# Second layer: queries' rms scale applied to the scores by row, keys' sums of squares as two fp32r products

## The reference

```python
for g, (window, dilation) in enumerate(B_PATTERNS):      # 3 groups
    q = apply_partial_rotary(rms_norm(qkv[:, :, 0, g], q_gain[g]), cos, sin)
    k = apply_partial_rotary(rms_norm(qkv[:, :, 1, g], k_gain[g]), cos, sin)
    o, lse = dilated_window_attention(q, k, qkv[:, :, 2, g], window // dilation, dilation)
...
wgt = jax.nn.softmax(jnp.stack(lses), axis=0)
y = o.reshape(bsz, S, B_WIDTH).astype(h.dtype) * jax.nn.silu(z)
```

## Time and profile before

| | |
|---|---|
| Median of 3 runs | 3209.98 us (3209.97 to 3212.14) |
| The profiled execution | 3211.42 us, of which its span 3209.7 us |
| PE busy | 98% |
| POOL, DVE, ACT busy | 49%, 50%, 34% |
| Second layer in the trace | about 425 to 1012 us |
| Mean granted clock of PE | 0.993 |

### The profile page before, as it was taken

How to read it: one execution, slowest core, us unless ns; L and a number is a source line. 1 busy time by engine, 2 the same in 40 slices (tenths; PEclk the granted TensorE clock), 3 DMA queues, 4 the chain that set the end, 5 groups by cost and what they waited for, 6 DMA issues and landing times.

```text
span 3209.7 us, 39426 instructions
## 1 busy us (share of the span) xinstructions
PE 3135.8 (98%) x16286; PEld 2596.1 (81%) x16286; DVE 1619.7 (50%) x2100; ACT 1106.7 (34%) x1509; POOL 1568.7 (49%) x1138
## 2 busy tenths in 40 slices
PE   8999999999999999999999999889999999999998
PEld 7988878788887888898887888766888777778887
DVE  6753565748373535345356777745121366551123
ACT  3221244444443322332223444434222343242222
POOL 4444466658473555444433422236454565345444
PEclk9999999999999999999999999999999999999999
DMA  5554422222222333255443211112323242213231
GB/s 168 164 171 142 139 92 76 79 66 79 74 85 63 95 101 97 92 171 180 135 158 128 66 40 40 40 48 84 105 92 96 89 142 81 79 62 96 92 105 66
DMA packets 279172, 319.33 MB, mean 99 GB/s; under 512 B 6850, under 2 KB 245073, under 8 KB 278674
## 3 DMA queue, kind: packets, MB, share of 16 engines
q1 hardware_dynamic: 240960, 247.48, 23.8%
q10 hardware_dynamic: 38034, 69.34, 6.3%
HBM read 310.50 MB, written 6.29 MB: 99 GB/s over the span
## 4 chain that ended last, share of the span: by engine, by line
PE 89%; DVE 5%; ACT 2%; POOL 2%; issue 1%; DMA 1%; ACTq 0%; SPq 0%; DVEq 0%
PE ps L550 25%; PE ps L551 25%; PE ps L552 25%; PE psx L755 1%; PE psx L1034 1%; POOL Wl L358 1%; PE ps L1065 1%; PE psx L734 1%; PE psx L649 1%; DVE tmp L1908 1%; PE psx L701 1%; PE psx L1193 1%; DVE stD L2282 1%; PE psx L797 1%; PE psx L795 0%
## 5 line engine op out<-in xcount | busy, mean ns | idle before, releaser
L358 POOL TENSOR_TENSOR Wl<-Wr,Wh 128x512 fp32r<-128x512 f32 x928 | 1282.8, 1413 | 1426.0 <-ACT Wh L1281 1421.9
L550 PE MATMUL ps<-Ah,Wh 128*128 128x512 f32 x1944 | 778.2, 400 | 0.7 <-POOL Wl L358 0.7
L552 PE MATMUL ps<-Ah,Wl 128*128 128x512 f32 x1944 | 757.7, 390 | 0.0
L551 PE MATMUL ps<-Al,Wh 128*128 128x512 f32 x1944 | 757.2, 390 | 0.0
L1281 ACT ACTIVATE Wh<-Wr 128x2048 fp32r<-128x2048 f32 x232 | 442.9, 1909 | 285.4 <-DMA Wr<-in_w_mlp_in_dram 109.9
L550 PEld LDWEIGHTS ps<-Ah,Wh 128*128 128x128 f32 x1944 | 365.2, 188 | 83.5 <-issue 9.2
L551 PEld LDWEIGHTS ps<-Al,Wh 128*128 128x128 f32 x1944 | 365.2, 188 | 82.1 <-issue 8.9
L550 PE MATMUL ps<-Yh,Wh 128*128 128x512 f32 x1088 | 426.3, 392 | 5.2 <-POOL Wl L358 5.2
L552 PEld LDWEIGHTS ps<-Ah,Wl 128*128 128x128 f32 x1944 | 364.8, 188 | 77.3
L551 PE MATMUL ps<-Yl,Wh 128*128 128x512 f32 x1088 | 424.3, 390 | 0.0
L552 PE MATMUL ps<-Yh,Wl 128*128 128x512 f32 x1088 | 424.3, 390 | 0.0
(11 more groups left out here) (399 smaller groups left out, 3907.7 us busy)
## 6 DMA issues: line engine op xcount, KB each, us to landing
Wr<-in_a_w_in_dram SPq DMA_DIRECT2D x48, 1024.0 KB, 6.6
modw<-in_w_mod_dram ACTq DMA_DIRECT2D x96, 512.0 KB, 5.5
Wr<-in_b_w_in_dram SPq DMA_DIRECT2D x40, 1024.0 KB, 5.0
Wr<-in_w_mlp_in_dram SPq DMA_DIRECT2D x32, 1024.0 KB, 5.6
Wr<-in_w_mlp_out_dram SPq DMA_DIRECT2D x32, 1024.0 KB, 5.1
Wr<-in_a_w_out_dram SPq DMA_DIRECT2D x16, 1024.0 KB, 5.2
Wr<-in_c_w_in_dram SPq DMA_DIRECT2D x16, 1024.0 KB, 5.7
Wr<-in_attn_w_qkv_dram SPq DMA_DIRECT2D x12, 1024.0 KB, 5.1
```

Source lines behind the costliest of these rows:

```text
L358: last = pool.tensor_tensor(E.Wl[:, s, part], E.Wr[:, s, part], E.Wh[:, s, part].bitcast(F32), ALU.subtract)
L550: pe.matmul(o, ah, bh, start=first, stop=False)
L551: pe.matmul(o, ah, bl, start=False, stop=False)
L552: return pe.matmul(o, al, bh, start=False, stop=last)
```

## The change

Queries are no longer scaled by their root mean square before the scores. ACT writes tile times gain straight into `QB`. The scale is a number per token, and the tokens of the queries are the rows of the scores, so it multiplies the scores by row. For that, the sums of squares are made in four blocks of 32 output partitions, one for each quarter of the tokens (one root for 128 columns instead of 512), a transpose (`columns`) puts tokens on the partitions, and DVE's `rate` takes the reciprocal of 4 columns into `stB`. In `scores`, three products by group replace the one instruction (the scale differs by group), and the maximum is an instruction of its own.

Keys keep their scale. Their squares are rounded to fp32r on ACT (`sh`), DVE subtracts to get the rest (`square_low`), and two fp32r products (high and rest) replace the fp32 product. `rsR` and `sqR` are the memory of `rs` and `sq` under the type fp32r.

DVE's order by step t becomes: `square_low(t)` for a key or `turn(t)` for a query; then, if t - 1 is a key, `scaled(t - 1)` and `turn(t - 1)`; then, if t - 2 is a query, `rate(t - 2)`. The diff, cut to its core:

```diff
+def is_key(t):
+    return t // 2 % 2 == 1
...
         def ssq(i, t):
             r = t % 2
             into(4 + r)
-            pe.wait_ge(*A.of("B", "sq", i, t))
-            pe.matmul(psx[:, r, :], ones[:], sq[:, r, :], start=True, stop=True).then_inc(*X.did("B", "ssq", i, t))
-            emptied[4 + r] = A.of("B", "sqrt", i, t)
+            if is_key(t):
+                pe.wait_ge(*V.of("B", "sl", i, t))
+                for half in (E.rsR, E.sqR):
+                    m = pe.matmul(psx[:, r, :], E.onesR[:], half[:, r, :], start=(half is E.rsR), stop=(half is E.sqR))
+                emptied[4 + r] = A.of("B", "sqrt", i, t)
+            else:
+                pe.wait_ge(*A.of("B", "sq", i, t))
+                for q in range(TT):
+                    m = pe.matmul(psx[32 * q:32 * q + 32, r, 0:P], ones[:, 0:32], sq[:, r, q * P:(q + 1) * P], start=True, stop=True)
+                emptied[4 + r] = V.of("B", "rq", i, t)
+            m.then_inc(*X.did("B", "ssq", i, t))
+
+        def columns(i, t):
+            r = t % 2
+            pe.wait_ge(*A.of("B", "sqrt", i, t))
+            pe.transpose(psx[:, r, P:2 * P], rs[:, r, 0:P], ident[:]).then_inc(*X.did("B", "rt", i, t))
...
             if t:
                 ssq(i, t - 1)
+            if t >= 2 and not is_key(t - 2):
+                columns(i, t - 2)
...
         def sqrt(i, t):
             r = t % 2
+            n = S if is_key(t) else P
             act.wait_ge(*X.of("B", "ssq", i, t))
-            if t >= 2:
+            if t >= 2 and not is_key(t):
                 act.wait_ge(*V.of("B", "qk", i, t - 2))
...
-            act.activation(tmp[:, t % 3, :], ps[t % 3][:], ACT.Copy).then_inc(*A.did("B", "cp", i, t))
+            if is_key(t):
+                n = t // 4 * 2 + t % 2
+                act.wait_ge(*A.of("B", "sq", i, t))
+                act.wait_ge(*X.of("B", "rt", i, t - 2))
+                act.activation(E.rsR[:, t % 2, :], sq[:, t % 2, :], ACT.Copy).then_inc(*A.did("B", "sh", i, t))
...
+                act.activation(tmp[:, n % 3, :], ps[t % 3][:], ACT.Copy).then_inc(*A.did("B", "cp", i, t))
+            else:
...
+                act.activation(E.QB[:, t // 4, t % 2, :], ps[t % 3][:], ACT.Identity, scale=pk(E, "b_q_gain", t // 4)).then_inc(*A.did("B", "cp", i, t))
...
-        def rest(i, t):
+        def square_low(i, t):
+            r = t % 2
+            dve.wait_ge(*A.of("B", "sh", i, t))
+            dve.tensor_tensor(E.sqR[:, r, :], sq[:, r, :], E.rsR[:, r, :].bitcast(F32), ALU.subtract).then_inc(*V.did("B", "sl", i, t))
...
+        def rate(i, t):
+            dve.wait_ge(*X.of("B", "rt", i, t))
+            dve.reciprocal(rq(t // 4, t % 2), psx[:, t % 2, P:2 * P].rearrange("p (q n) -> p q n", q=TT)[:, :, 0]).then_inc(*V.did("B", "rq", i, t))
+
+        def scaled(i, t):
...
+        def turn(i, t):
...
-            dve.tensor_tensor_reduce(PB[:, u % 2, :], psx[:, u % 2, :], maskB[:, u % 4, :], 1.0, 10 * NEG,
-                                     ALU.add, ALU.max, stB[:, u, 0:1]).then_inc(*V.did("B", "sc", i, u))
...
+            for g, c0, c1 in ((0, 0, 256), (1, 256, 384), (2, 384, 512)):
+                dve.scalar_tensor_tensor(PB[:, u % 2, c0:c1], psx[:, u % 2, c0:c1], rq(g, u // 4)[:, u % 4:u % 4 + 1], maskB[:, u % 4, c0:c1],
+                                         ALU.mult, ALU.add).then_inc(*V.did("B", "sc", i, u))
             dve.wait_ge(*V.of("B", "sc", i, u))
+            dve.tensor_reduce(stB[:, u, 0:1], PB[:, u % 2, :], AX.X, ALU.max).then_inc(*V.did("B", "mx", i, u))
...
-            for t in range(11):
-                rest(i, t)
-                if i and t == 1:
+            for t in range(13):
+                if t < 12:
+                    if is_key(t):
+                        square_low(i, t)
+                    else:
+                        turn(i, t)
+                if t and is_key(t - 1):
+                    scaled(i, t - 1)
+                    turn(i, t - 1)
+                if 2 <= t and not is_key(t - 2):
+                    rate(i, t - 2)
+                if i and t == 2:
                     y(i - 1, 1)
-            rest(i, 11)
```

More of the change, by code:

```diff
@@ L216, in setting @@
     E.Wh = sb("Wh", [P, SLOTS, 2048], F32R)
-    E.ones, E.ident = sb("ones", [P, P]), sb("ident", [P, P])
+    E.onesR, E.ident = sb("onesR", [P, P], F32R), sb("ident", [P, P])
+    E.ones = E.onesR[:].bitcast(F32)
     E.PK = sb("PK", [P, NCOL])
@@ L224, in setting @@
     E.rc = sb("rc", [P, 2, TT])
+    E.rsR, = phase(("rsR", [P, 2, S], F32R))
     E.rs = sb("rs", [P, 2, S])
+    E.sqR, = phase(("sqR", [P, 2, S], F32R))
     E.sq = sb("sq", [P, 2, S])
@@ L532, in pe_program @@
     T, X, A, V, G, LO = E.T, E.X, E.A, E.V, E.G, E.LO
-    x, tmp, tmpf, sq, rc, ones, ident, psx, psf = E.x, E.tmp, E.tmpf, E.sq, E.rc, E.ones, E.ident, E.psx, E.psf
+    x, tmp, tmpf, sq, rc, rs, ones, ident, psx, psf = E.x, E.tmp, E.tmpf, E.sq, E.rc, E.rs, E.ones, E.ident, E.psx, E.psf
     Ah, Al, Yh, Yl = E.Ah, E.Al, E.Yh, E.Yl
@@ L1454, in mixer_b @@
         PB, stB, ropeB = E.PB, E.stB, E.ropeB
-        qf = E.QB[:].rearrange("p a b n -> p (a b n)")
+        kf = E.KB[:].rearrange("p a b n -> p (a b n)")
         LDB = E.signals["ld_b"]
@@ L1464, in sqrt @@
             r = t % 2
+            n = S if is_key(t) else P
             act.wait_ge(*X.of("B", "ssq", i, t))
-            if t >= 2:
+            if t >= 2 and not is_key(t):
                 act.wait_ge(*V.of("B", "qk", i, t - 2))
-            act.activation(rs[:, r, :], psx[:, r, :], ACT.Sqrt, bias=eps[:, 0:1], scale=1.0 / P).then_inc(*A.did("B", "sqrt", i, t))
+            act.activation(rs[:, r, 0:n], psx[:, r, 0:n], ACT.Sqrt, bias=eps[:, 0:1], scale=1.0 / P).then_inc(*A.did("B", "sqrt", i, t))
         def qk(i, t):
@@ L1476, in qk @@
             act.activation(sq[:, t % 2, :], ps[t % 3][:], ACT.Square).then_inc(*A.did("B", "sq", i, t))
[L1477 to L1480, removed]
-            act.activation(tmp[:, t % 3, :], ps[t % 3][:], ACT.Copy).then_inc(*A.did("B", "cp", i, t))
+            if is_key(t):
[3 more added lines that the diff above has]
+                act.activation(E.rsR[:, t % 2, :], sq[:, t % 2, :], ACT.Copy).then_inc(*A.did("B", "sh", i, t))
+                if n >= 3:
+                    act.wait_ge(*V.of("B", "qk", i, t - (5 if t % 2 else 7)))
+                elif i:
+                    act.wait_ge(*X.of("B", "pv", i - 1, 0))
+                act.activation(tmp[:, n % 3, :], ps[t % 3][:], ACT.Copy).then_inc(*A.did("B", "cp", i, t))
+            else:
+                if i and t == 0:
+                    act.wait_ge(*X.of("B", "s", i - 1, 7))
+                act.activation(E.QB[:, t // 4, t % 2, :], ps[t % 3][:], ACT.Identity, scale=pk(E, "b_q_gain", t // 4)).then_inc(*A.did("B", "cp", i, t))
             if t % 2 == 0:
@@ L1969, in preamble @@
     def preamble():
-        dve.memset(E.ones[:], 1.0).then_inc(*V.did("ones"))
+        dve.memset(E.acc[:], 1.0).then_inc(*V.did())
+        dve.wait_ge(*V.now())
+        dve.tensor_copy(E.onesR[:], E.acc[:, 0:P]).then_inc(*V.did("ones"))
         dve.memset(eps[:], EPS).then_inc(*V.did("eps"))
@@ L2084, in rest @@
             dve.wait_ge(*A.of("B", "cp", i, t))
-            if i and t == 0:
-                dve.wait_ge(*X.of("B", "s", i - 1, 7))
-            dve.scalar_tensor_tensor(dst, tmp[:, t % 3, :], pk(E, "b_k_gain" if qk else "b_q_gain", g), rs[:, r, :],
+            dve.scalar_tensor_tensor(KB[:, t // 4, t % 2, :], tmp[:, n % 3, :], pk(E, "b_k_gain", t // 4), rs[:, r, :],
                                      ALU.mult, ALU.mult).then_inc(*V.did("B", "qk", i, t))
-            dve.wait_ge(*V.of("B", "qk", i, t))
+        def turn(i, t):
+            dst = (KB if is_key(t) else QB)[0:32, t // 4, t % 2, :]
+            dve.wait_ge(*(V.of("B", "qk", i, t) if is_key(t) else A.of("B", "cp", i, t)))
             if t >= 2:
@@ L2093, in rest @@
                 dve.wait_ge(*X.of("B", "pv", i - 1, 0))
-            swapped = (acc if r else tmp[:, 3, :])[0:32, :]
+            swapped = (acc if t % 2 else tmp[:, 3, :])[0:32, :]
             pinned()
-            dve.stream_shuffle(swapped, dst[0:32, :], SWAP).then_inc(*V.did("B", "swap", i, t))
+            dve.stream_shuffle(swapped, dst, SWAP).then_inc(*V.did("B", "swap", i, t))
             dve.wait_ge(*V.of("B", "swap", i, t))
```

15 lines of the change are left out of this document (9 added, 6 removed).

## The result

The changed kernel takes 3267.51 us (median of 4 runs, 3264.51 to 3272.05) against 3211.06 (median of 4 runs, 3209.97 to 3213.63) for the kernel before on the same chip: a ratio of 1.0176 [1.0158, 1.0193], slower by 56 us. The profiled run took 3272.05 us, 60.6 more than the profiled run of before; it is the slowest of the four, 4.5 us above their median.

The account below looks back on a forecast made before the run. PE was taken as the bound, with DVE and POOL close behind. The terms -15.5 (PE work) + 48.6 (waits) + 26.4 (clock) + 4.4 (scores) gave +63.9 us: 3274 us for the median, 8-in-10 range 3232 to 3296.

Parts of the forecast that it names:

- the likeliest case: PE waits for `rate` at 12 odd keys and the clock falls: 3257 to 3293 us by short and long waits, chance 0.58.
- PE work (15.5 forecast): Sums of squares on PE: key pairs 0.46 for 0.86 us, query block plus transpose 0.62 for 0.86; gains 9.7 and 5.8.
- The waits (48.6 forecast: PE before the odd key's sum, waiting for DVE's `rate`: 8 x 4.15 + 4 x 3.85 us; 34 short, 59 long.
- I take 1.6: Duration of `square_low` on DVE in the chain to `rate`: 1.6 us, range 0.6 to 1.8.
- The clock (26.4 forecast): Granted clock falls behind PE's waits: 2.2 us each, x12; ends 0 and 30.
- The scores (4.4 forecast): DVE's three products plus maximum lengthen the chain 1.1 us per unit; exposed at unit 4, 4 x 1.1 us.
- The rule on the tiling mode: Query blocks on PE: changing tiling mode drains the engine; query gains 5.8 us with the drain, some 11 without.
- that the clock would stay up: Rival: waits as worked out but no clock fall, +37.5 or +23; 3247 or 3233 us, chance 0.22.
- That the fp32r pairs would run at the pace of fp32: Rival at the key's sum: the 9.7 us are not gained, the waits stay; 3284 us, chance 0.04.
- That POOL would be late: Rival: weight splits queue behind late rotations, PE waits there too, 2 us more each; +16, 3290 us, chance 0.09.
- the prediction's signs of being wrong: In the profile after: no wait for `rate`, one under 3 us, or PE waiting for weight splits inside the layer.
- The faster rival: DVE reaches `rate` before PE asks, chain from E under 6.1 us instead of 10.25: 3199 us, chance 0.05.

Follow-up runs that it names:

- experiment 2: Changed kernel with DVE's `rate(t - 2)` ahead of `scaled(t - 1)` and `turn(t - 1)`, and the turns in ascending order as well: 3202.63 us, ratio 0.9967.
- experiment 4: Changed kernel with `rate` ahead and turns ascending, but the key's sum again one fp32 product, no rounded copy or `square_low`: 3211.07 us, ratio 0.9996.
- experiment 6: Changed kernel, order kept, with 12 unused fp32r products into an idle bank ahead of PE's wait for `rate` at each odd key: 3245.6 us, ratio 1.0105.
- experiment 3: Changed kernel with DVE's turns in ascending order alone, `rate` left behind `scaled` and `turn`: 3257.77 us, ratio 1.0132.
- experiment 1: Changed kernel with DVE's `rate(t - 2)` moved ahead of `scaled(t - 1)` and `turn(t - 1)`, nothing else: 3244.54 us, ratio 1.0101.
- experiment 7: Changed kernel with 5 unused fp32r products (1.15 us) ahead of PE's wait for `rate` at each odd key: 3254.39 us, ratio 1.0136.

## Why the prediction was right

The time came out at 3267.5 where 3274 was forecast, within the likeliest case (12 waits and a fall of the clock, 3257 to 3293; its short and long waits alone give 3259 and 3284, the rest of those ends was not worked out). The mechanism was the one forecast. Step by step:

- **PE work (15.5 forecast).** The pair takes 0.46 us, as forecast; block and transpose 0.61 for 0.62, the block 0.44 for 0.47. Experiments 2 and 4 give 8.4 us for the keys in measured time where the sum has 9.7, with runs that scatter by 3 and 6 us; their traces give 9.6 for the keys and 5.6 for the queries (5.8 forecast), 15.2 in all.
- **The waits (48.6 forecast, 40.6 measured).** This is the mis-sized term. Place, number and releaser are as forecast, none stands at an even key, but the twelve are 2.83 to 4.11 us long, 3.38 on average for 4.05. To the 40.6 come 12 x 0.16 = 1.9: PE's idle time is counted from the end of the last product, drawn 0.39 long, where a product holds PE for 0.229. So 42.5 are to be held against 48.6. The chain starts as forecast: for the first wait the square root at E + 0.66 and `square_low` at E + 2.54 (2.55 forecast). `rate` starts at E + 10.03 there (10.1 forecast, 10.25 for its end). The step that failed is "I take 1.6" for `square_low`: the twelve in front of the odd keys took 1.26 on average, which is 4.0 us of the missing 6.1. The reciprocal, gain product, shuffle and multiply behind it took 5.73 instead of 5.93, another 2.4. The group of all 24, and two of them:

```profile
L2116 DVE TENSOR_TENSOR sqR<-sq,rsR 128x512 fp32r<-128x512 f32 x24 | 30.8, 1284 | 83.0 <-ACT rsR L1505 83.0
```

```profile
613.28 0.69 DVE L2116 TENSOR_TENSOR sqR<-sq,rsR 128x512 fp32r<-128x512 f32 x1 [4.32 <-ACT rsR L1505]
...
794.94 1.82 DVE L2116 TENSOR_TENSOR sqR<-sq,rsR 128x512 fp32r<-128x512 f32 x1 [5.06 <-ACT rsR L1505]
```

  The mean is 1.28, from 0.69 with POOL idle (the wait behind that one is 2.83 us) to 1.82 with POOL at work (wait 4.11). POOL was at work beside it at nine of the twelve odd keys, but that alone does not give the price. This subtraction, of an even key, took 0.69 us too, and the instruction of POOL that starts 0.05 us behind it took 1.80 instead of some 1.3:

```profile
757.60 0.69 DVE L2116 TENSOR_TENSOR sqR<-sq,rsR 128x512 fp32r<-128x512 f32 x1 [3.75 <-ACT rsR L1505]
757.65 1.80 POOL L423 TENSOR_TENSOR QB<-QB,acc 32x512 f32<-32x512 f32 x1
```

  The one of 1.82 started at 794.94, 0.07 us behind an instruction of POOL that ran until 796.16. In 19 of the 24 places an instruction of POOL was running when the subtraction started, and the subtraction ended 0.55 to 0.61 us behind that instruction (in two places, on the change between two of POOL's, behind the second). In the other five it took 0.69. So the price goes from 0.69 to 1.89 by which of the two starts first and by how much, and no single number fits twelve places.
- **The clock (26.4 forecast).** It fell behind eleven of twelve waits. Stretches of one us behind each wait give 50 us of PE at 1.2 GHz, 25 us lost; experiment 6 gives 22 in another way. Per fall that is 2.3 us (2.2 forecast), from 1.5 to 3.1. That it was eleven is in part luck: behind the twelve waits of experiment 3, nearly as long (2.72 to 3.75 us), it fell eight times.
- **The scores (4.4 forecast).** The wait for normalised weights went from 1.1 to 4.5 us, +3.4. DVE's timeline of one unit:

```profile
568.58 1.00 DVE L2161 SCALAR_TENSOR_TENSOR PB<-psx,stB,maskB 128x256 f32<-128x256 f32 x3 [3.65 <-PE psx L820]
569.62 0.69 DVE L2164 TENSOR_REDUCE stB<-PB 128x1 f32<-128x512 f32 x1
570.34 0.15 DVE L2166 TENSOR_SCALAR stB<-stB 128x1 f32<-128x1 f32 x1
```

  The three products took 1.00 us, above the 0.79 worked out from the earlier trace rows and also above the 0.91 by the Trainium skill's page VectorE: DVE Perf Modes, section The TRN2 errata. Behind them the waits that I had put at 0.15 each took 0.04 and 0.03. From the first product to L2166 are 1.76 us, and in the kernel before 554.69 - 553.96 = 0.73, from the start in the earlier trace rows to this line of the same timeline:

```profile
554.69 0.15 DVE L2115 TENSOR_SCALAR stB<-stB 128x1 f32<-128x1 f32 x1
```

  So the chain is 1.03 longer (1.1 forecast): two sizes were off and cancelled. The wait grew by 3.4 and not by 4 x 1.03 = 4.1 because the chain starts earlier: its first product starts 0.75 us after PE begins L820 of that unit (567.83), where the one instruction of before started 0.93 after L797 (553.03).
- **The rule on the tiling mode.** The block costs 0.44 us for 0.22 of streaming at the pace of fp32, so entering and leaving take 0.22, as the row of before had it and as the drain of the Trainium skill's TensorEngine Tiling (Array Packing), section Key Properties, would have it. No run here changes columns without changing the mode, so the drain itself is not shown.
- **The sum.** The same product, the one ahead of the out projection, starts at 1025.41 before and here, in the changed kernel:

```profile
1081.52 0.79 PE L558 MATMUL ps<-Yh,Wh 128*128 128x512 f32 x1 [5.16 <-POOL Wl L366]
```

  The layer is 56.1 us longer. The pieces give 40.6 + 1.9 + 25 + 3.4 + 0.5 - 15.5 = 55.9, where the 0.5 us are one wait for a weight split. The 15.5 are the forecast; with the 15.2 of the traces they give 56.2. The profiled spans differ by 60.3 us. The last 4 arise behind the layer, where nothing was changed and PE's waits add up to the same within 1 us. They fit the clock: PE works 45 us at 1.2 GHz there against 34 before, 5.6 us lost. The same 50 us of the program, 56 us later in the changed kernel:

```profile
2100.00:2150.00 50.00, 43.27 (x207) 32.86 (x206) 23.58 (x36) 17.92 (x27) 15.42 (x13) 0.93 0.13 43
```

```profile
2156.00:2206.00 50.00, 43.10 (x194) 31.89 (x194) 22.53 (x35) 17.28 (x26) 11.22 (x9) 0.86 0.13 43
```

  Over the twelve traces this part takes 2182.2 to 2189.9 us, so 4 us there say nothing of the change.
- **The rivals.** That the clock would stay up is refuted by the stretches. That the fp32r pairs would run at the pace of fp32 is refuted by the 0.46 us of the pair. That POOL would be late was right in its mechanism and hidden in this kernel: 0.5 us of it can be seen as long as `rate` is late (by the letter one of the prediction's signs of being wrong, at a thirtieth of the 16 us that it had for this case), since PE's own waits give POOL time; experiment 1 brings it out. The faster rival ("the chain from E to `rate` under 6.1 us") names what experiment 2 then did, and its 3199 us are 3.6 away from it.

## What to carry to other kernels

A tiny instruction that frees a buffer inherits the lateness of everything queued ahead of it in its engine: put the release first, then look again, since the next late thing is often another order on the same engine. Keep the order in which two engines hand tiles to each other the same on both; one pair out of order cost 42 us here. Where PE is the bound, a stall costs its length and here about half as much again by the clock (25 us on 41 in the changed kernel, 14 on 26 in experiment 1, 16 on 37 in experiment 3), and work taken off PE counts only if the engine that takes over the preparation has room: 2.4 us for four tiles were there, 3.6 were asked.

## What the runs showed of the hardware that was not expected

- The granted clock and the length of a gap: it fell behind gaps of 1.83 and 1.84 us and not behind 2.99 (experiment 7) or 3.10 us (the changed kernel). In experiment 1 a pair of gaps of 0.75 and 1.42 us stands at the same place of the second, third and fourth pass; the clock fell behind the pair in the second and not in the two others. The stretches behind the pairs of the second and third pass:

```profile
630.00:634.00 4.00, 4.00 (x12) 3.08 (x12) 3.86 (x3) 0.60 (x2) 3.84 (x4) 0.59 0.27 95
779.50:783.50 4.00, 4.00 (x18) 3.31 (x19) 3.73 (x3) 0.73 (x2) 3.92 (x3) 1.00 0.33 115
```

- The time at 1.2 GHz behind a wait in the changed kernel was between 2.9 and 6.2 us, and it does not go by the length of the wait: 6.2 us behind one of 3.33, 3.4 us behind one of 3.28.
- The same subtraction of two SBUF tiles takes DVE 0.69 us with POOL idle, or where it starts just ahead of POOL's instruction, and up to 1.89 where it starts just behind one. The reciprocal, with one input, takes 3.34 beside POOL (457.78) and 3.35 without it (613.89), so the cost of the neighbour depends on the instruction. The Trainium skill, SBUF — State Buffer, section SBUF: two separate sides, says the same: DVE and GpSimd block one another where the DVE instruction has two SBUF inputs. The prediction had the two prices, but took one of them for all twelve places.
